# Expert blocks of a streaming encoder layer: the transposes of x between the up and gate products, the first half of h transposed one gate step sooner, the second half behind six down products

## The reference, cut to what matters

```python
D_MODEL = 1024
N_EXPERTS = 32
D_EXPERT = D_MODEL // 2
ROW_BLOCK = 128
...
    def expert_block(args):
        xe, e = args
        return (jax.nn.silu(xe @ w_g[e]) * (xe @ w_u[e])) @ w_d[e]

    yb = lax.map(expert_block, (xb, block_e))
    out = jnp.zeros((T + 1, h.shape[1]), jnp.float32).at[row_tok].add(
        yb.reshape(P, h.shape[1]).astype(jnp.float32) * row_w[:, None])
```

## Time and profile before

| what | value |
|---|---|
| time, median of 3 runs (lowest to highest) | 2204.78 us (2203.3 to 2205.7) |
| time of the profiled execution | 2202.57 us |
| its span | 2200.8 us |
| TensorE busy over the span | 2088.1 us (95%) |
| expert blocks, from the first up product to the last down product | 1368.9 to 2191 us |
| mean granted TensorE clock over the span | 0.977 |

### The profile page before, as it was taken

How to read it: one execution, slowest core, us unless ns; L and a number is a source line. 1 busy time by engine, 2 the same in 40 slices (tenths; PEclk the granted TensorE clock), 3 DMA queues, 4 the chain that set the end, 5 groups by cost and what they waited for, 6 DMA issues and landing times. The chain is left out here.

```text
span 2200.8 us, 40164 instructions
## 1 busy us (share of the span) xinstructions
PE 2088.1 (95%) x13505; PEld 1771.5 (80%) x13506; DVE 1623.4 (74%) x2083; ACT 1260.0 (57%) x2200; POOL 806.9 (37%) x689
## 2 busy tenths in 40 slices
PE   8999999995899999899999895999999999999998
PEld 6888888884687887678787774888888888888887
DVE  3799999984777667867878967969698556556644
ACT  5322433335677777866676643768588555456533
POOL 1111544553566654545545435222222222222221
PEclk9999999996999999999999996999999999999999
DMA  7553344334333242333222117989899968767852
GB/s 228 186 191 134 118 128 159 120 106 144 114 117 109 80 131 81 108 105 116 80 73 92 54 70 258 361 281 372 308 357 373 329 197 282 228 198 264 285 172 35
DMA packets 211517, 393.17 MB, mean 179 GB/s; under 512 B 54749, under 2 KB 81757, under 8 KB 211389
## 3 DMA queue, kind: packets, MB, share of 16 engines
q1 hardware_dynamic: 197853, 357.42, 47.1%
q0 software_dynamic: 13536, 34.12, 6.8%
HBM read 315.42 MB, written 91.23 MB: 185 GB/s over the span
## 5 line engine op out<-in xcount | busy, mean ns | idle before, releaser
L2428 DVE TENSOR_TENSOR p_w_lo<-p_raw,p_w_hi 128x1024 fp32r<-128x1024 f32 (+1 forms) x260 | 439.5, 1728 | 150.5 <-ACT p_w_hi L2223 149.9
L2051 POOL TENSOR_TENSOR p_wgt<-p_wgt,p_past 128x1024 f32<-128x1024 f32 (+4 forms) x166 | 308.5, 1859 | 347.2 <-DVE p_past L1929 347.1
L2223 ACT ACTIVATE p_w_hi<-p_raw 128x2048 fp32r<-128x2048 f32 (+1 forms) x198 | 361.8, 1859 | 84.0 <-PE p_up L2310 67.3
L762 DVE SCALAR_TENSOR_TENSOR p_ut<-p_ut,p_cw 128x512 f32<-128x512 f32 (+1 forms) x480 | 329.2, 762 | 0.0
L1929 DVE TENSOR_TENSOR_SCAN p_past<-p_keep,p_past,p_one 128x513 f32<-128x513 f32 (+1 forms) x196 | 225.9, 1193 | 75.3 <-ACT p_keep L1746 73.3
L1746 ACT ACTIVATE p_keep<-p_zp 128x512 f32<-128x512 f32 (+3 forms) x326 | 158.8, 547 | 119.2 <-PE p_zp L1620 106.5
L2310 PE MATMUL p_gp<-p_w_hi,p_xt_hi 128*128 128x256 f32 x736 | 210.4, 286 | 0.0
L436 PE MATMUL p_pj<-p_w_hi,p_xt_hi 128*128 128x512 f32 x512 | 205.2, 401 | 4.2 <-DVE p_xt_lo L738 2.4
L2310 PE MATMUL p_gp<-p_w_lo,p_xt_hi 128*128 128x256 f32 x736 | 206.5, 281 | 0.0
L2310 PE MATMUL p_gp<-p_w_hi,p_xt_lo 128*128 128x256 f32 x736 | 206.4, 280 | 0.0
L436 PE MATMUL p_pj<-p_w_hi,p_xt_lo 128*128 128x512 f32 x512 | 200.6, 392 | 0.0
(11 more groups left out here) (309 smaller groups left out, 4975.6 us busy)
## 6 DMA issues: line engine op xcount, KB each, us to landing
p_raw<-in_w_up SPq DMA_DIRECT2D x128, 512.0 KB
p_raw<-in_w_gate SPq DMA_DIRECT2D x128, 512.0 KB
p_raw<-in_w_down SPq DMA_DIRECT2D x128, 512.0 KB
wide_raw<-in_w_in SPq DMA_DIRECT2D x56, 256.0 KB, 3.8
wide_raw<-in_x SPq DMA_DIRECT2D x17, 512.0 KB
scr_y<-wide_raw SPq DMA_DIRECT2D x17, 512.0 KB, 3.1
wide_raw<-scr_y SPq DMA_DIRECT2D x17, 512.0 KB
y_out<-wide_raw SPq DMA_DIRECT2D x17, 512.0 KB, 2.9
```

The costliest lines, as they stand in the source:

```text
L762: dve.scalar_tensor_tensor(dst, src, cw[:, a, j:j + 1], dst, ALU.mult, ALU.add).then_inc(tap_done, 1)
L2051: pool.tensor_tensor(mine, mine, past_rows[:, u % NP, 0:n, 2:2 + w], ALU.mult).then_inc(a_done, 1)
L2223: act.activation(part(w_hi, p, wide), raw[:, n % RING:n % RING + wide, :], ACT.Copy).then_inc(whi_done, wide)
L2428: dve.tensor_tensor(part(w_lo, p, wide), raw[:, n % RING:n % RING + wide, :], part(w_hi, p, wide).bitcast(F32), ALU.subtract).then_inc(wlo ...
```

## The change

Three pieces of TensorE's list in the block are moved; nothing is added or taken away, and the lists of the other engines are left as they are.

```diff
                     hidden(up[:, :], 0, 0, FF, range(KT)).then_inc(up_done, 1)
+                    transpose_x(b + 1)
                     weights(e, 2)
                     hidden(gp[:, 0, 0:HF], 1, 0, HF, range(KT)).then_inc(g_done[0], 1)
-                    hidden(gp[:, 1, 0:HF], 1, HF, FF, range(5))
+                    hidden(gp[:, 1, 0:HF], 1, HF, FF, range(4))
                     transpose_h(b, 0)
-                    hidden(gp[:, 1, 0:HF], 1, HF, FF, range(5, KT)).then_inc(g_done[1], 1)
-                    transpose_x(b + 1)
+                    hidden(gp[:, 1, 0:HF], 1, HF, FF, range(4, KT)).then_inc(g_done[1], 1)
                     weights(e, 3)
                     pe.wait_ge(hl_done[0], b + 1)
                     pe.wait_ge(yo_done, b)
-                    down(0, (0,))
+                    down(0, (0, 1))
                     transpose_h(b, 1)
-                    down(0, (1,))
                     down(1, (0, 1))
```

## The result

| what | before | after |
|---|---|---|
| median (7 runs each, taken together) | 2203.31 us (2201.18 to 2205.7) | 2211.95 us (2209.38 to 2214.48) |
| ratio after to before, 95% interval | | 1.0039 (1.0029 to 1.0048) |
| time of the profiled execution | 2202.57 us | 2209.38 us |
| expert phase, start of the first up product to start of the last down product | 822.0 us | 832.3 us |

The account below looks back on a forecast made before the run. TensorE's unbroken row of work bounds the expert phase; 31 x (0.35 + 0.06) = 12.7, 15 x (0.06 - 0.10) = -0.6 and -0.67 give +11.4 on 2202.57, 2214.0. With the median 2.2 higher: 2216.2 us, 8 in 10 for 2210.5 to 2219.5.

Parts of the forecast that it names:

- Which wait, where and how often: TensorE waits for VectorE's ht_lo at the first down product, in the 31 of 46 blocks where ScalarE converts pairs of pieces.
- Its price: At the first down product: a wait of 0.35 us, with the 0.10 saving at the switch to down lost.
- g: Start of the last product of the first gate half; ht_lo is ready at g + 3.24, down can start at g + 3.50.
- The other margins: Cover left at TensorE's transposes of h and its down products: 0.11, 0.07 and 0.09 us, so no wait there.
- rival B: A second wait opens: h's second half waits up to 0.08 us in all 46 blocks, +3.7 us, 2220; 11 in 100.
- The first gather: GpSimd's gather in the first block could land 1.2 us late, once; taken as 0.
- The earlier step of h: First-half transposes of h one gate step sooner: 0.11 us cover in blocks without pieces, otherwise a 0.25 us wait.
- The switch costs: First products behind transposes run slower: +0.06 us at gate in every block, -0.10 at down where TensorE doesn't wait.
- rival A: Gate products run faster behind transposes, 0.114 us instead of 0.118: +6.4 us in all, 2211; 12 in 100.
- The Trainium skill's 109 ns: Page's pace for 256 column gate products, against 0.118 us traced; using it would give a sum of about -1 us.
- The 0.67 us of the late piece: Taken away once: the pair of pieces late in the 18.54 us block would be in time in longer blocks.
- The sum: Wait, switch costs and late piece over all blocks: +11.4 us on the profiled execution, 2214.0; 70 in 100.

Follow-up runs that it names:

- ladder of two and four transposes: Changed kernel with two or four of the eight transposes of x back between gate and down: 2207.6 us (1.0012) and 2202.4 us (0.9992).
- pair split: Changed kernel, ScalarE's pair of pieces behind the first silu converted singly, one ahead of and one behind h's high part: 2197.8 us, 0.9971.
- both sets of transposes together: Changed kernel with the transposes of x right ahead of those of h's first half, inside the second gate half: 2203.6 us, 1.0005.
- both pairs first: Changed kernel with both of ScalarE's pairs of pieces converted ahead of its first silu: 2199.4 us, 0.9976.

## Why the prediction was right, step by step

**Which wait, where and how often: right.** The wait appears at the first down product for ht_lo, in the 31 blocks with pieces and in no other place. Its cause is shown by taking the pair apart with the transposes of x where they are, and by the ladder of two and four transposes. One reading was too generous: 1486.14 is the start of the transposes of h and not their end, which is 1486.52, only 0.14 us ahead of ht_hi. That the pair came last and not they is known from the split.

**Its price: right.** The sum set 0.35 for the wait and 0.10 for the slow start behind it, 0.45. The pair split measures 0.46 to 0.47: without the pair the first down product starts 0.38 us sooner (g + 3.11 in place of g + 3.49), and the first takes 0.23 to the next in place of 0.31.

**The other margins: right.** The 0.07 to 0.11 us of cover held in all 46 blocks; rival B did not happen. The two ahead of down products were read well: 0.12 and 0.09 in the changed kernel. The one ahead of the transposes is larger than I had it, since a transpose that had to wait starts 0.06 behind its operand and not 0.26. The first gather cost nothing: in the first block the transposes of x start 0.23 behind the last up product, without a wait.

**The earlier step of h: right.** I wrote that without it blocks without pieces would wait 0.25. With x alone moved they take 18.22 us, where the whole change has 17.78. Of this 0.44, 0.15 is the second wait, for h (the chain above), and the rest is the first one with its slow start: the first down product starts 1.51 us behind the start of the transposes of h, as forecast, where without a wait it would be 1.28 (1.63 in the changed kernel, less three products at 0.118). The two moves of h earn their place together; neither was run by itself.

**The switch costs: wrong, the loss and the gain.** "+0.06 in every block" for the switch to gate and "-0.10" for the one to down were read from the start to start of the first products, 0.20 and 0.31. But the last transpose ahead of them lasts only 0.03 to the next start, and 0.03 + 0.20 is 0.109 + 0.118. The row splits the same time at another place. A switch costs 0.01 or less: the kernel with both sets of transposes together, which has one switch fewer, is no faster.

**The pace of gate: rival A, in part, and some luck.** The blocks without pieces came out at 17.78, not 17.82. The 36 gate products behind the transposes of x take 4.11 us in the changed kernel, 0.114 each, where 39 took 4.59 before; the last 12 run at 0.118. So A's mechanism is there for three quarters of the gate products. With switches at nothing, the blocks without pieces would have stayed at 17.86 us, and those with pieces would be at 17.86 + 0.46; the pace takes 0.08 off both kinds. The sum came within 0.04 us of both by luck: it had a gain from switches where there is a gain from pace. Rival A's 2211 is no better founded, though the median stands beside it: its terms were 0.33 and -0.21 us a block, and 0.38 and -0.08 were measured. The Trainium skill's 109 ns ("TensorE: Matmul & The Clock Gate", "Back-to-back issue gap"), which the section gives for an isolated matmul, was reached in none of the kernels; the measured 0.113 to 0.118 decide.

**The 0.67 us of the late piece: right in size, wrong in kind.** I took it away because longer blocks need less of the DMAs. It is absent from the second trace of the unchanged program too, so nothing shows it to be a saving of the change.

**The sum.** 31 x 0.38 = 11.8, 15 x -0.08 = -1.2, -0.7 once, and 0.3 from the first block (18.30 us) and rounding, make the 10.2 us by which the phase grew from trace to trace; against the second trace of the kernel before (823.1 us) it is 9.2. The median says 8.6, with an interval of 6.4 to 10.6. What lies outside the phase ran 1377.1 us in the profiled execution after and 1380.5 and 1379.6 in the two of before, though the change doesn't touch it; over the twelve traces it goes from 1376.2 to 1382.1. That spread covers the difference between phase and median.

## What to carry to other kernels

In a row of work without any wait, an instruction that seems free to move may be the cover of a chain on two other engines. Before moving it, count for each hand-over behind it what is ready when, and what stands in the other engines' lists inside that chain: here a conversion of 1.91 us that nobody on the path needed. When the move is wanted for other reasons, move or split that conversion too: with the pair split, the changed kernel runs in 0.9971 (0.9960 to 0.9983) of the time of the one before, 2197.8 us, the lowest median of all that were run (both pairs first is too near to be told from it: 0.9976, 0.9966 to 0.9987). The split by itself gains nothing (0.9997); what the two kernels gain over the one before comes from the pace of gate, in the next section, and not from the cover.

## What the runs showed that I had not expected

The pace of 256 column products has two levels, 0.118 and 0.114 us (0.113 in the fastest rows), at the same granted clock of 1.00. With eight transposes of x right behind up, the first gate products, up to the transposes of h, ran at the fast one in 42 to 46 of the 46 blocks (4.11 us for 36), with six there in 35 (4.10). With four there (in 45 blocks) or with the transposes elsewhere they ran at the slow one (4.24). In the changed kernel 4 of 46 blocks kept the slow pace, with the same instructions. This is where the gain of the two fastest kernels over the one before comes from, some 0.1 us a block, and behind the transposes of h it differed between two executions of one program. What sets it stays open; no run was made that could tell.

An engine that had to wait starts at different distances: a down product 0.25 us after the last operand's end, a transpose 0.06 (in the blocks without pieces with x alone moved, and in the one block that waited with both pairs first).
